# A two-layer hybrid attention step in fp32 on one Trainium2 core: RMS norms by half tiles, squared and summed beside the products before them

## The chip, the cores and the metric

The kernel runs on one core of a Trainium2 chip, as one launch. The metric is device time in microseconds (us); lower is better. Everything is fp32 apart from a few masks.

## The reference, cut to what matters

A trunk of two layers works on 512 prompt tokens and 8 sample tokens, 1024 channels each. The change concerns the RMS norm alone, which is applied five times: before the mixers and before the feed-forward part in both layers, and once at the end.

```python
def rmsnorm(x, g):
    xf = x.astype(jnp.float32)
    y = xf * lax.rsqrt(jnp.mean(xf * xf, axis=-1, keepdims=True) + RMS_EPS)
    return (y * g.astype(jnp.float32)).astype(x.dtype)
...
for i in range(DEPTH):
    h = rmsnorm(x, norm_mix_g[i])      # then all input projections read h
    x = x + merge_branches(...)        # ends in the product with w_out
    h = rmsnorm(x, norm_ffn_g[i])      # then gate and up read h
    x = x + swiglu(h, ...)             # ends in the product with w_down
y = rmsnorm(x, norm_final_g)
```

The loop is a summary; the rest of the layer (three attention branches over a paged past, gates, log-forget values) is as before in every respect.

## The kernel before, in words

**Layout.** The residual stream lies transposed in `xT`: 8 tiles of 128 channels by 520 tokens. A norm needs, for each token, the sum of squares over all 8 tiles and 128 partitions. The normalised stream goes to `hT`. [...]

**Order of work.** Five engines run hand-written programs that meet at semaphores. TensorE (PE), ScalarE (ACT) and VectorE (DVE) each run, per layer, norm 0, `project`, `compress`, `attend`, `merge`, norm 1, `ffn`. SyncE (SP) issues all loads in one fixed order: weights come in chunks of up to 2 MB through a ring of three slots, and a slot is loaded again once its last reader has signalled. GpSimd (POOL) scales probabilities, and forms sums and differences of weight blocks, in `merge`, `out`, `ffn` and `down`; these are two-input operations from SBUF.

**Products by seven.** The large products are done as a 2x2 block scheme with 7 products in place of 8 (helper `seven`, L1034; its `product` at L1042 is 4 matmuls of 260 columns). For the output projection and for gate and up it runs the groups f_1, f_11, d, f_u, f_22, f_21, f_12, each for q = 0 and 1. The d group multiplies a weight sum (POOL) with the difference of two quarters of the input, for `ffn` the tile BT[0], made by `first_sum` (L1936) on DVE; `later_sums` makes the other three (L1868 to L1870). The output projection runs `seven` twice (hf = 0, 1), and DVE adds each finished product to `xT` (L1922).

**Down projection** (`long`, L1163): four columns n = 0 to 3, each of seven products of 11 matmuls, p_1, p_2, d, p_6, p_3, p_7, p_4. DVE adds each to `xT` (L1991). The last one, p_4, completes tile 2n+1, half 0.

**The norm.** ACT squares whole tiles of 520 columns (L1234) into two buffers; PE multiplies each with a matrix of ones, two matmuls a tile (L603, L604), 16 in all, which adds over partitions and, in PSUM, over tiles; ACT takes two square roots (L1237); for each half DVE takes a reciprocal (L1594) and writes 8 tiles of `hT` (L1597, `scalar_tensor_tensor` with the gain). In the norm before `ffn` DVE makes `first_sum` after half of the second half's tiles. `project` computes its tile 0 first for token half 0 and then for half 1 (L653), waiting tile by tile of `hT`; its other tiles take both halves (L648, L649), and the first rotation is L626. At the very end PE transposes `hT` back (L582), which is then stored.

At the start SP loads constants and x, PE transposes x, DVE copies it to `xT` (L1585, L1586), and the first 2 MB of input weights follow (L464).

## Time and profile before

| | us |
|---|---|
| median of 3 runs | 2884.73 |
| lowest and highest | 2883.32, 2887.96 |
| the profiled execution, its own time | 2888.6 |
| its span, first to last instruction | 2886.8 |
| PE busy | 2584.5 (90%) |
| DVE, ACT, POOL busy | 897.1, 538.7, 638.0 |
| mean granted PE clock | 0.935 of full |

In the trace's views a line shows when a group of equal instructions started, how long it lasted, and in brackets how long its engine had been idle and who released it. A PE matmul record of 260 columns lasts 0.38 us, but the next starts 0.22 us after it.

### The profile page before, as it was taken

How to read it: one execution, taken by the hardware profiler on the slowest of the kernel's cores; microseconds unless marked ns; L12 is line 12 of the kernel's file. 1: busy time of each engine (PE TensorE's matmuls, PEld its weight loads, DVE VectorE, ACT ScalarE, POOL GpSimd, SP SyncE). 2: the span in 40 equal slices, each digit the busy share in tenths (PEclk: the TensorE clock that was granted, in tenths of full speed). 3: DMA queues.
4: the chain of work that ended last, by engine and by line, in shares of the span. 5: the costliest groups of instructions: out<-in, count | busy, mean ns of one | idle time of the engine just before them, and what ended most of it. 6: DMA issues, size and time to landing. Idle time of an engine off the chain costs nothing.

```text
span 2886.8 us, 43032 instructions
## 1 busy us (share of the span) xinstructions
PE 2584.5 (90%) x13546; PEld 1991.7 (69%) x13546; DVE 897.1 (31%) x1801; ACT 538.7 (19%) x1356; POOL 638.0 (22%) x564
## 2 busy tenths in 40 slices
PE   5997788877899999999999878888689999999997
PEld 4885544444588878888888664444357887888886
DVE  2203455421222432233131145552112334223412
ACT  1013222212222111110010232222141220111100
POOL 0000012111132424443300001121111242444431
PEclk8999789877999999999999998997789999999998
DMA  6242334245122212222514233341532222222120
GB/s 190 82 127 73 91 103 120 72 117 156 67 88 88 88 59 88 88 70 71 161 52 137 62 105 100 110 125 40 171 101 88 87 79 68 87 82 83 64 81 30
DMA packets 288295, 270.89 MB, mean 94 GB/s; under 512 B 50882, under 2 KB 249746, under 8 KB 287810
## 3 DMA queue, kind: packets, MB, share of 16 engines
q1 hardware_dynamic: 271266, 258.43, 29.2%
q10 hardware_dynamic: 16800, 9.61, 1.1%
q8 instruction: 119, 1.95, 0.3%
q14 instruction: 110, 0.90, 0.1%
HBM read 258.36 MB, written 17.97 MB: 96 GB/s over the span
## 4 chain that ended last, share of the span: by engine, by line
PE 77%; SPq 8%; issue 5%; DVE 5%; ACT 2%; POOL 1%; DMA 1%; ACTq 0%; DVEq 0%; POOLq 0%
PE ps L1042 32%; PE ps L1163 8%; PE ps L582 6%; PE ps L648 5%; PE ps L649 5%; SPq L557 3%; PE ps L938 3%; PE ps L863 2%; PE ps L802 2%; SPq L554 2%; POOL ring L1495 1%; PE ps L759 1%; PE ps L614 1%; PE ps L613 1%; PE ps L716 1%
## 5 line engine op out<-in xcount | busy, mean ns | idle before, releaser
L1495 POOL TENSOR_SCALAR ring<-ring,rr,gnat 128x31 f32<-128x31 f32 (+2 forms) x192 | 100.6, 534 | 1063.8 <-DVE rr L1713 1063.8
L1042 PE MATMUL ps<-hT,ring 128*128 128x260 f32 x1344 | 307.2, 386 | 8.2 <-DVE hT L1597 8.2
L1042 PEld LDWEIGHTS ps<-hT,ring 128*128 128x128 f32 x1344 | 258.2, 192 | 49.4 <-DVE hT L1597 9.0
L582 PE MATMUL ps<-cst,units 128*128 128x128 f32 x960 | 161.3, 302 | 61.2 <-ACT arena L1314 16.8
L1042 PE MATMUL ps<-hT,units 128*128 128x260 f32 x928 | 213.2, 382 | 0.0
L648 PE MATMUL ps<-hT,ring 128*128 128x260 f32 x672 | 202.4, 383 | 0.0
L649 PE MATMUL ps<-hT,ring 128*128 128x260 f32 x672 | 202.1, 382 | 0.0
L1042 PEld LDWEIGHTS ps<-hT,units 128*128 128x128 f32 x928 | 176.3, 190 | 27.1
L582 PEld LDWEIGHTS ps<-cst,units 128*128 128x128 f32 x960 | 114.6, 152 | 103.9 <-ACT arena L1314 38.0
L582 PE MATMUL ps<-cst,ring 128*128 128x128 f32 (+1 forms) x464 | 104.7, 314 | 75.9 <-POOL ring L1495 36.8
L1042 PE MATMUL ps<-arena,units 128*128 128x260 f32 x704 | 157.9, 382 | 0.0
L582 PEld LDWEIGHTS ps<-cst,ring 128*128 128x128 f32 (+1 forms) x464 | 54.9, 147 | 138.6 <-issue 72.5
L1042 PEld LDWEIGHTS ps<-arena,units 128*128 128x128 f32 x704 | 133.8, 190 | 20.5
L1788 DVE COPY arena<-ps 128x512 f32<-128x512 f32 x176 | 120.0, 687 | 88.4 <-PE ps L582 86.6
L649 PEld LDWEIGHTS ps<-hT,ring 128*128 128x128 f32 x672 | 127.7, 190 | 19.6
L648 PEld LDWEIGHTS ps<-hT,ring 128*128 128x128 f32 x672 | 126.3, 191 | 18.3
L1532 POOL TENSOR_TENSOR units<-ring 128x512 f32<-128x512 f32 x44 | 59.8, 1358 | 338.4 <-PE ps L1042 338.4
L1510 POOL TENSOR_TENSOR units<-ring 128x512 f32<-128x512 f32 x32 | 40.5, 1267 | 385.5 <-PE ps L1042 270.8
L1441 ACT ACTIVATE arena<-ps 128x260 f32<-128x260 f32 x132 | 51.1, 387 | 362.5 <-PE ps L1042 362.5
L1006 PE MATMUL ps<-units,arena 128*32 128x256 f32 x256 | 87.9, 506 | 33.2 <-DMA units<-in_cache_sb_kv 25.6
L1700 DVE TENSOR_REDUCE nm<-ps 128x2 f32<-128x256 f32 (+2 forms) x112 | 72.8, 650 | 140.4 <-PE ps L768 132.9
L1338 ACT ACTIVATE ring<-ps,nm 128x128 f32<-128x128 f32 (+2 forms) x224 | 100.3, 454 | 21.7 <-DVE nm L1700 21.2
(319 smaller groups left out, 4381.5 us busy)
## 6 DMA issues: line engine op xcount, KB each, us to landing
ring<-in_w_in SPq DMA_DIRECT2D x20, 2048.0 KB, 7.9
units<-in_cache_fox_kv SPq DMA_DIRECT2D x256, 128.0 KB, 2.2
units<-in_cache_sb_kv SPq DMA_DIRECT2D x256, 128.0 KB, 2.2
ring<-in_w_ffn_gate SPq DMA_DIRECT2D x22, 1024.0 KB, 5.4
ring<-in_w_ffn_up SPq DMA_DIRECT2D x22, 1024.0 KB, 8.0
ring<-in_w_ffn_down SPq DMA_DIRECT2D x16, 1408.0 KB, 6.2
units<-in_cache_nsa_cmp_kv SPq DMA_DIRECT2D x128, 128.0 KB, 2.6
units<-in_cache_nsa_sel_kv SPq DMA_DIRECT2D x256, 64.0 KB, 1.8
```

The costliest lines, as they stand in the source:

```text
L557: dma(slot[:, j * cols:(j + 1) * cols], rows(name)[l * NPOOL + pg][:, c0:c0 + cols]).then_inc(sem, 16)
L582: return nc.tensor.transpose(o, i, ident[0:n, 0:n])
L648: mm(ps[:, 2 * (i % 2), 0:H2], w[:, k, j * P:(j + 1) * P], hT[:, k, 0:H2], start=k == 0, stop=k == KD - 1)
L649: last = mm(ps[:, 2 * (i % 2) + 1, 0:H2], w[:, k, j * P:(j + 1) * P], hT[:, k, H2:T], start=k == 0, stop=k == KD - 1)
L938: mm(ps[lo, bank, :], qa, KT[0][:, i % 2, :], start=first, stop=True, skip_group_check=True).then_inc(sems["smm_a"], 1)
L1006: fox = mm(bank[64:96, 0:256], PTf[:, 4 * h + j, :], sf[:, j, :], start=h == 0 and j == 0, **sk)
L1042: last = mm(ps[:, bank, 0:H2], w[:, k, :], a[:, k, :], start=first and k == 0, stop=True, skip_group_check=True)
L1163: last = mm(ps[:, bank, 0:H2], w[:, k, :], x[k] if x is D2 else x[:, k, :], start=first and k == 0, stop=True, skip_group_check=True)
L1338: last = fn(Pb[:, n % 2, hh, 0:w], ps[:, hh, 0:w], ACT.Exp, bias=nm[:, n % 2, hh:hh + 1], accum_out=sm[:, n % 2, hh:hh + 1])
L1495: last = nc.gpsimd.tensor_scalar(p, p, one, gnat[:, i, c:c + 1], ALU.mult, ALU.mult)
L1700: v.tensor_reduce(nm[:, n % 2, :], ps[:, 0:2, 0:w], AX.X, ALU.max, negate=True).then_inc(sems["nm_ready"], 1)
L1788: v.tensor_copy(KT[s][:, i % 2, :], bank).then_inc(sems["kt_ev"], 1)
```

## The change

**Squares by half tiles.** ACT now squares 16 half tiles of 260 columns per norm, in the order in which the products before complete them (`HALVES`), each as soon as its last add has been made. DVE adds 12 of them into one running sum per token half (`accumulate`); the first square of a half is written straight into the sum, and the last is left to PE.

**PE's part** shrinks from 16 matmuls to 4: `total` multiplies the running sum and the last square of one half with ones. One half's `total` is put inside the product ahead of the norm (between the two f_12 products of the output projection; at k = 5 of the last p_4), the other behind the first product that follows (f_1 of `ffn`; the first 8 matmuls of `project`).

**The norm itself** begins with the half whose squares are complete; DVE makes the very last residual add after two tiles of that half (`early`). `project` computes tiles 0 and 1 for half 1 and then for half 0. The norm before a layer is now issued at the end of the layer before. At the start, x goes to another place, and `posT` is copied after the norm. The change's short description also names an overlap of the last two stick-breaking heads with the up projections; the kernel before has one in its plan (`in_order`), and no edit touches it.

```diff
+HALVES = ([(2 * n + c, h, name, k) for n in range(4)
+           for c, h, name, k in ((0, 0, "r_2", n + 1), (0, 1, "x_upd", 2 * n + 1), (1, 1, "r_d", n + 1), (1, 0, "x_upd", 2 * n + 2))],
+          [(4 * hf + 2 * q + c, h, name, k + q) for hf in range(2)
+           for c, h, name, k in ((0, 0, "x_11", 2 * hf + 1), (1, 1, "d_22", 2 * (NMG + hf) + 1), (1, 0, "x_upd", 4 * hf + 1), (0, 1, "x_upd", 4 * hf + 3))
+           for q in range(2)])
...
+class Squares:
...
+        self.half = [x[1] for x in HALVES[w]]
+        ends = [[e for e in range(16) if self.half[e] == h] for h in range(2)]
+        self.first, self.last = [x[0] for x in ends], [x[-1] for x in ends]
+        held = [e for e in range(16) if e not in self.first]
+        self.place = {e: i % 4 for i, e in enumerate(held)}
+        summed = [e for e in held if e not in self.last]
+        self.nth = {e: i + 1 for i, e in enumerate(summed)}
+        self.before = {e: held[i - 4] for i, e in enumerate(held) if i >= 4}
+        self.previous = {e: max([f for f in summed if f < e and self.half[f] == self.half[e]], default=None) for e in summed}
+        self.all_summed = [max(self.nth[e] for e in summed if self.half[e] == h) for h in range(2)]
...
+            def total(l, w, h):
+
+                sums, bank = SQUARES[w], 6 * w + h
+                pe.wait_ge(sems["sq_used"], at(pe, "sq_used", l, 12 * w + sums.all_summed[h]))
+                mm(ps[:, bank, 0:H2], C("ones")[:, 0:P], sqsum[:, h], start=True, stop=False)
+                pe.wait_ge(sems["sq_ready"], at(pe, "sq_ready", l, 16 * w + sums.last[h] + 1))
+                mm(ps[:, bank, 0:H2], C("ones")[:, 0:P], sq[:, sums.place[sums.last[h]]], start=False, stop=True).then_inc(sems["sum_ps"], 1)
...
+                    for k in range(KD if i >= 2 else 0):
...
-                        for k in range(KD):
-                            pe.wait_ge(sems["h_ready"], at(pe, "h_ready", l, t * KD + k + 1))
-                            last = mm(ps[:, t, 0:H2], w[:, k, 0:P], hT[:, k, t * H2:(t + 1) * H2], start=k == 0, stop=k == KD - 1)
-                    last.then_inc(sems["proj_ps"], 1)
+                    for t in (1, 0) if i == 0 else ():
+                        for m in range(2):
+                            for k in range(KD):
+                                if m == 0:
+                                    pe.wait_ge(sems["h_ready"], at(pe, "h_ready", l, (1 - t) * KD + k + 1))
+                                last = mm(ps[:, 2 * m + t, 0:H2], w[:, k, m * P:(m + 1) * P], hT[:, k, t * H2:(t + 1) * H2], start=k == 0, stop=k == KD - 1)
+                            if t == 0:
+                                last.then_inc(sems["proj_ps"], 1)
+                            elif m == 0:
+                                total(l, 0, 0)
+                    if i >= 2:
+                        last.then_inc(sems["proj_ps"], 1)
...
                     product(3 * q, w1[q][:, :, lo], x(0), True).then_inc(sems["f_1"], 1)
+                    if q == 0:
+                        between("first")
...
                     product(3 * q + 2, ws[q][3], x(3)).then_inc(sems["f_12"], 1)
+                    if q == 0:
+                        between("last")
...
-                    seven(l, 2 * (NMG + hf), w1, w2, [[MS[q][0], MS[q][1], w1[q][:, :, P:2 * P], MS[q][2]] for q in range(2)], 4, merged, OT_, free)
+                    seven(l, 2 * (NMG + hf), w1, w2, [[MS[q][0], MS[q][1], w1[q][:, :, P:2 * P], MS[q][2]] for q in range(2)], 4, merged, OT_, free,
+                          lambda part: total(l, 1, 0) if hf and part == "last" else None)
...
-                            if bank == "b":
-                                pe.wait_ge(sems["rs_ready"], at(pe, "rs_ready", l, 4))
...
-                    seven(l, 2 * (NMG + NOUT + j), w1, w2, ws, 8, quarter, BT, free)
+                    seven(l, 2 * (NMG + NOUT + j), w1, w2, ws, 8, quarter, BT, free,
+                          lambda part: total(l, 1, 1) if j == 0 and part == "first" else None)
...
+                    long(f, w2[:, :, hi], D4, True, lambda k: total(l.next, 0, 1) if n == 3 and k == 5 else None).then_inc(sems["p_4"], 1)
+
+            total(0, 0, 1)
...
-            norm(DEPTH, 0)
+            total(DEPTH, 0, 0)
...
-                    fn(sq[:, k % 2, :], xT[:, tile, :], ACT.Square).then_inc(sems["sq_ready"], 1)
...
-                for t in range(2):
-                    fn(rs[:, t * H2:(t + 1) * H2], ps[:, t, 0:H2], ACT.Sqrt, bias=epsb[:, 0:1], scale=1.0 / D).then_inc(sems["rs_ready"], 1)
...
+                def square(e):
+                    t, h, name, n = HALVES[w][e]
+                    act.wait_ge(sems[name], at(act, name, l, n) if w else count(act, l, PER[name], n))
+                    if e in sums.before:
+                        act.wait_ge(sems["sq_used"], at(act, "sq_used", l, 12 * w + sums.nth[sums.before[e]]))
+                    fn(sq[:, sums.place[e]] if e in sums.place else sqsum[:, h], xT[:, t, h * H2:(h + 1) * H2], ACT.Square).then_inc(sems["sq_ready"], 1)
+
+                def take_root(n, h):
+                    act.wait_ge(sems["sum_ps"], at(act, "sum_ps", l, 2 * w + n))
+                    fn(rs[:, h], ps[:, 6 * w + h, 0:H2], ACT.Sqrt, bias=epsb[:, 0:1], scale=1.0 / D).then_inc(sems["rs_ready"], 1)
+
+                for e in range(15):
+                    square(e)
+                take_root(1, 0 if w else 1)
+                square(15)
+                take_root(2, 1 if w else 0)
...
+            norm(0, 0)
...
+                norm(l.next, 0)
...
+                    dve.wait_ge(sems["sq_used"], at(dve, "sq_used", l, 12 * w + sums.nth[sums.previous[e]]))
+                to = sqsum[:, sums.half[e]]
+                v.tensor_tensor(to, to, sq[:, sums.place[e]], ALU.add).then_inc(sems["sq_used"], 1)
...
+                v.tensor_copy(xT[:, k, 0:SEQ], ps[:, 2 * (k % 2), :]).then_inc(sems["x_upd" if k % 2 else "r_2"], 1)
+                v.tensor_copy(xT[:, k, SEQ:T], ps[:, 2 * (k % 2) + 1, 0:NS]).then_inc(sems["r_d" if k % 2 else "x_upd"], 1)
+                if k:
+                    accumulate(0, 0, 2 * k - 2)
+                    accumulate(0, 0, 2 * k - 1)
+
+            def norm(l, w, g, early=lambda: None, amid=lambda: None):
+                for n, t in enumerate((0, 1) if w else (1, 0)):
+                    dve.wait_ge(sems["rs_ready"], at(dve, "rs_ready", l, 2 * w + n + 1))
+                    own(v.reciprocal(ps[:, 6 + t, 0:H2], rs[:, t]), "rinv_ok", l, 2 * w + n + 1)
                     for k in range(KD):
                         to = slice(t * H2, (t + 1) * H2)
                         v.scalar_tensor_tensor(hT[:, k, to], xT[:, k, to], g(k), ps[:, 6 + t, 0:H2], ALU.mult, ALU.mult).then_inc(sems["h_ready"], 1)
...
+                        if n == 0 and k == 1:
+                            early()
+                        if n and k == KD // 2 - 1:
                             amid()
...
                     add("f_1", 0, 0, a, "c_1")
-                    add("f_11", 0, 0, b, None, "c_1")
+                    add("f_11", 0, 0, b, "x_11", "c_1")
+                    if hf:
+                        squares(-2, 0)
                     add("f_u", 0, 1, a, "c_u")
+                    squares(0, 2)
                     add("f_22", 1, 1, a, "c_3")
                     add(None, 1, 1, d, "d_22", "c_3")
-                    add("f_21", 1, 0, a, "x_upd")
-                    add("f_12", 0, 1, d, "x_upd", "c_u")
+                    add("f_21", 1, 0, a, "x_upd", None, (0,))
+                    squares(2, 4)
+                    add("f_21", 1, 0, a, "x_upd", None, (1,))
+                    squares(4, 5)
+                    add("f_12", 0, 1, d, "x_upd", "c_u", (0,))
+                    squares(5, 7 if hf else 6)
+                    if hf:
+                        norm(l, 1, lambda k: gl[:, 0, k:k + 1], lambda: add("f_12", 0, 1, d, "x_upd", "c_u", (1,)), lambda: first_sum(l))
+                    else:
+                        add("f_12", 0, 1, d, "x_upd", "c_u", (1,))
...
                     add(x12, d).then_inc(sems["x_upd"], 1)
+                    accumulate(l.next, 0, 4 * n)
+                    accumulate(l.next, 0, 4 * n + 1)
...
                     add(x22, d).then_inc(sems["r_d"], 1)
-                    dve.wait_ge(sems["p_4"], at(dve, "p_4", l, n + 1))
-                    add(x21, f).then_inc(sems["x_upd"], 1)
...
+                    def finish():
+                        dve.wait_ge(sems["p_4"], at(dve, "p_4", l, n + 1))
+                        add(x21, f).then_inc(sems["x_upd"], 1)
+
+                    if n < 3:
+                        accumulate(l.next, 0, 4 * n + 2)
+                        finish()
+                        accumulate(l.next, 0, 4 * n + 3)
+                    else:
+                        norm(l.next, 0, lambda k: gl[:, 1, k:k + 1], finish)
+
+            norm(0, 0, lambda k: gam[:, 0, k:k + 1])
...
+                dve.wait_ge(sems["h_ready"], at(dve, "h_ready", l, 2 * KD))
+                v.tensor_copy(gl[:, :, :], gam[:, bass.ds(2 * i + 1, 2), :])
```

## Rows read from the trace of the kernel before

**Rows 1.** The page: busy time by engine, and the chain that ended last by engine

```profile
PE 2584.5 (90%) x13546; PEld 1991.7 (69%) x13546; DVE 897.1 (31%) x1801; ACT 538.7 (19%) x1356; POOL 638.0 (22%) x564
...
PE 77%; SPq 8%; issue 5%; DVE 5%; ACT 2%; POOL 1%; DMA 1%; ACTq 0%; DVEq 0%; POOLq 0%
```

**Rows 2.** Timeline, layer 0's second norm: start, length, engine, line, op, count, [idle before]

```profile
1024.65 1.92 PE L1042 MATMUL ps<-PT,vnat 128*128 128x260 f32 x8
1024.94 0.42 DVE L1922 TENSOR_TENSOR xT<-xT,ps 128x260 f32<-128x260 f32 x1 [1.43 <-PE ps L1042]
...
1026.87 1.27 POOL L1532 TENSOR_TENSOR units<-ring 128x512 f32<-128x512 f32 x1 [19.73 <-PE ps L1042]
...
1027.48 0.64 ACT L1234 ACTIVATE arena<-xT 128x520 f32<-128x520 f32 x1 [27.83 <-PE ps L604]
...
1033.34 0.60 PE L604 MATMUL ps<-arena,cst 128*128 128x260 f32 x2
1033.98 0.85 ACT L1237 ACTIVATE arena<-ps,epsb 128x260 f32<-128x260 f32 x2 [1.24 <-PE ps L604]
...
1034.49 1.79 DVE L1594 RECIPROCAL ps<-arena 128x260 f32<-128x260 f32 x1 [7.36 <-ACT arena L1237]
1035.85 1.26 POOL L1539 TENSOR_TENSOR units<-ring,units 128x512 f32<-128x512 f32 x1 [0.16 <-POOL units L1536]
1036.31 3.26 DVE L1597 SCALAR_TENSOR_TENSOR hT<-xT,gl,ps 128x260 f32<-128x260 f32 x8
...
1038.04 8.69 PE L1042 MATMUL ps<-hT,ring 128*128 128x260 f32 x32 [4.10 <-DVE hT L1597]
...
1041.50 0.39 ACT L1441 ACTIVATE arena<-ps 128x260 f32<-128x260 f32 x1 [6.68 <-PE ps L1042]
1043.00 1.24 DVE L1936 TENSOR_TENSOR arena<-hT 128x1040 f32<-128x1040 f32 x1
...
1046.56 7.18 PE L1042 MATMUL ps<-arena,units 128*128 128x260 f32 x32
```

**Rows 3.** Timeline, the same stretch of layer 1

```profile
2427.98 1.92 PE L1042 MATMUL ps<-PT,vnat 128*128 128x260 f32 x8
...
2451.36 7.18 PE L1042 MATMUL ps<-arena,units 128*128 128x260 f32 x32
```

**Rows 4.** Timeline, end of layer 0 and first projections of layer 1

```profile
1444.28 4.79 PEld L1163 LDWEIGHTS ps<-arena,ring 128*128 128x128 f32 x22
...
1444.70 1.22 DVE L1991 TENSOR_TENSOR xT<-xT,ps 128x260 f32<-128x260 f32 x3 [3.94 <-PE ps L1163]
...
1460.07 8.97 PE L653 MATMUL ps<-hT,ring 128*128 128x260 f32 x32 [2.91 <-DVE hT L1597]
...
1475.66 0.41 PEld L626 LDWEIGHTS ps<-PT,cst 128*128 128x128 f32 x2
```

**Rows 5.** Timeline, the final norm

```profile
2847.39 4.79 PEld L1163 LDWEIGHTS ps<-arena,ring 128*128 128x128 f32 x22
...
2868.04 2.39 PE L582 MATMUL ps<-cst,hT 128*128 128x128 f32 x10 [7.90 <-DVE hT L1597]
```

**Rows 6.** Timeline, the first projection of layer 0

```profile
49.58 9.68 PE L653 MATMUL ps<-hT,ring 128*128 128x260 f32 x32 [7.73 <-DMA ring<-in_w_in]
...
65.89 0.19 PEld L626 LDWEIGHTS ps<-PT,cst 128*128 128x128 f32 x1
```

**Rows 7.** A stretch: busy time by engine, then granted clock as a share of full

```profile
1038.00:1040.00 2.00, 1.96 (x5) 1.58 (x6) 2.00 (x5) 0.00 (x0) 0.00 (x0) 0.50 0.00 0
```

**Rows 8.** Duration in ns, min/median/max, of one DVE line

```profile
L1951 DVE TENSOR_TENSOR PT<-arena x66: 421/423/3120, 1058.0 to 2715.0; 128x260 f32<-128x260 f32 x66
```

**Rows 9.** Timeline, POOL beside that line's longest one

```profile
1309.89 3.17 POOL L1548 TENSOR_TENSOR units<-ring 128x1408 f32<-128x1408 f32 x1 [15.15 <-PE ps L1042]
1310.22 3.12 DVE L1951 TENSOR_TENSOR PT<-arena 128x260 f32<-128x260 f32 x1
```

**Rows 10.** Waits: engine, line, who released it, us in total, times, longest

```profile
DVE xT L1991 <- PE ps L1163: 214.5, 44, 9.2
```

More of the change, by code:

```diff
@@ L165, in __init__ @@
         self.more = more
+        self.next = Layer(more + 1) if more == 0 else None
 def w_dmas(ch):
@@ L344, in build @@
         VALUE_SEM = {"selv": "v_sel", "winv": "v_sel", "fxv": "v_fox", "sbv": "v_sb"}
-        CREDIT = {name: PER[name] for name in ("p_6", "p_4", "v_sel", "v_fox", "v_sb")}
+        CREDIT = {name: PER[name] for name in ("p_6", "p_4", "v_sel", "v_fox", "v_sb", "r_2", "r_d")}
         BASE = {"x_upd": KD}
@@ L1035, in so, with seven @@
                 last.then_inc(sems["so_ps"], 1)
-            def seven(l, g, w1, w2, ws, base, x, t, free):
+            def seven(l, g, w1, w2, ws, base, x, t, free, between=lambda part: None):
                 def product(bank, w, a, first=False):
@@ L1460, in _ @@
                 l = layer[0] = in_layers(act, i)
-                norm(l, 0)
                 project(l)
@@ L1913, in merge, with add @@
                     g = 2 * (NMG + hf)
-                    def add(name, t, h, bank, to, n=None):
-                        for q in range(2):
+                    def add(name, t, h, bank, to, n=None, only=(0, 1)):
+                        for q in only:
                             x = xT[:, 4 * hf + 2 * q + t, h * H2:(h + 1) * H2]
@@ L2018, in _ @@
                 merge(l)
-                norm(l, 1, lambda k: gl[:, 1, k:k + 1], lambda: first_sum(l))
                 ffn(l)
             assert chain[0] == DVE_CHAIN, chain
-            layer[0] = DEPTH
-            chain[0] = 0
-            norm(DEPTH, 0, lambda k: gam[:, 2 * DEPTH, k:k + 1])
             yp = PT[:, 0:8, :].rearrange("p a b -> p (a b)")[:, 0:4096].rearrange("p (t d) -> p t d", t=TT)
```

68 lines of the change are left out of this document (28 added, 40 removed).

## The prediction

> **What bounds the kernel now.** I read the page first [rows 1]: PE is busy 90% of the span and holds 77% of the chain that ended last. So time is won where PE stands still or does work that can go. The five norms are such places, and I read the timeline around each.
>
> The norm before `ffn` shows the pattern [rows 2]. PE begins the last product of the output projection (f_12, q = 1) at 1024.65. 1.75 us later, at 1026.40, it turns to ones-matmuls, and the last pair of these starts at 1033.34. ACT's root starts at 1033.98, DVE's reciprocal at 1034.49, the first tile of `hT` at 1036.31, and PE resumes at 1038.04. It then does four products, f_1 and f_11, and begins d at 1046.56. From 1024.65 to 1046.56 are 21.91 us. A product is 8 records, and one comes every 0.22 us (22 weight loads in 4.79 us, [rows 4]): 4 matmuls of 0.44, or 1.75 us. So five useful ones are 8.8 us and the norm costs PE 13.1 us. Layer 1 takes 23.38 us for the same stretch [rows 3].
>
> At the layer boundary [rows 4] the last p_4 begins at 1444.28, and project's tiles 0 and 1 are done at 1475.66: 31.38 us, of which 4.83 + 14.04 (11 and 32 matmuls) are useful. The final norm [rows 5] puts 20.65 us between the start of p_4 and the first transpose back. The first norm differs: there PE waits until 49.58 for the first weights, a DMA in the trace, after 7.73 us of idle [rows 6].
>
> **The change, part by part.** My links, all from rows 2, are these. From the start of a `total`'s weight load to the root is 1.30 us: 0.22, one matmul of 0.44, and the 0.64 from 1033.34 to 1033.98. From root to reciprocal is 0.51, from reciprocal to first `hT` tile 1.82. A further tile costs 0.41, its result is there 0.48 after its start, and an add to `xT` takes the same pipeline slot of 0.41. A `total` costs PE two matmuls, 0.88 us. The square of a half tile is not in the trace; it lies between ACT's copy of the same shape, 0.39 at 1041.50 [rows 2], and the 0.64 of a whole tile, at 1027.48. I take 0.39, the same engine and width.
>
> *Norm before `ffn`, layer 0.* The first `total` is put at 1024.43 (loads run 0.22 ahead of matmuls) and f_12 q = 1 moves to 1025.3. ACT must square the tile added at 1024.94 to 1025.36 before it takes the root, which therefore starts at 1025.8. Reciprocal at 1026.3, first tile at 1028.15; four tiles and the one late add in their midst are done at 1028.15 + 4 x 0.41 + 0.48 = 1030.3. PE resumes there instead of at 1038.04, 7.7 us earlier, after 2.8 us of standing still. Then f_1 (1.75), the second `total` from 1032.05, and f_1, f_11, f_11: PE is free at 1038.2. The second half's chain gives root 1033.35, reciprocal 1033.85, first tile 1035.7, four tiles 1037.4, and then `first_sum` of 1.24, as at 1043.00 in rows 2. POOL is late next: its weight sums for `ffn` start when f_12 ends and last 10.24 us (1026.87 to 1037.11). They move with f_12 by 0.88, to end at 1038.0. A DVE instruction with two SBUF operands waited for POOL's [rows 8, 9]: 3.12 us in place of 0.42. So I let `first_sum` wait till 1038.0 and end at 1039.3, d begins at about 1039.5, and 7.0 us are saved; in layer 1, whose old stretch is 1.47 longer, 8.5. The clock takes some back. PE had stood still for 4.10 us at 1038.04, and the granted clock of the next 2 us was 0.50, the 1.2 GHz level [rows 7]; the four products took 8.3 us (1038.04 to 1046.34, the load of d) instead of 7.0. After the 2.91 us ahead of 1460.07 [rows 4], 32 records took 8.97 us where 7.18 is usual, as at 1046.56 [rows 2]. At half rate, f_1 needs up to 3.5 us and the second `total` up to 1.76, which lies on the chain: up to 2.6 us each. I take 0.9 each. Sum for both: 15.5 - 1.8 = 13.7 us.
>
> The Trainium skill, "TensorE: Matmul & The Clock Gate", section "Why this matters for your kernels", says to leave no idle gap of some length between matmul bursts, or the clock goes to its lower level. Rows 7 agree that it fell after the old gap. By that rule alone the shorter gap would cost nothing and the sum would be 1.8 us larger.
>
> *Boundary.* The `total` inside p_4 loads at 1444.28 + 5 x 0.44 = 1446.47; the square it needs follows the adds at 1444.70 to 1445.92 and is done at 1446.35, so nothing waits. Root 1447.8, reciprocal 1448.3, first tile 1450.1. PE ends p_4 at 1450.0 (0.88 later than before) and starts project at 1450.6; it stops again before its third matmul, as the late add lies between tiles 2 and 3 (0.3), and ends the first 8 matmuls at 1454.5. The second `total` follows; its chain of 1.30 + 0.51 + 1.82 + 0.48 = 4.1 us is covered by that `total` and 8 matmuls, 4.4. Without this cover 0.3 us at most would come back. It and three more times 8 matmuls make: 1454.5 + 0.88 + 24 x 0.44 = 1465.9, against 1475.66. Saved: 9.8 us.
>
> *Final norm.* The same chain from 2847.39: first tiles 2853.2, late add done 2854.5, its square 2854.9, `total`, root 2856.2, but DVE writes the first half until 2857.0; reciprocal to 2858.8, tile at 2859.3, and PE transposes from there instead of 2868.04. Saved: 8.7 us. The transposes after it stay at low clock; were they not, up to 1.5 us more.
>
> *First norm.* PE starts at 49.58 in any case. It had no norm left after that; now one `total` of 0.88 stands between its products. Loss: 0.9 us. DVE's 12 adds ahead, 12 x 0.42 = 5 us, slow PE's transposes of x and are hidden by the 7.73 us of waiting; were that cover gone, they would cost their 5.
>
> *The 60 new adds on DVE* (12 per norm) and ACT's 80 half squares in place of 40 whole ones (80 x 0.39 = 31 us against 40 x 0.64 = 26, on an engine that waits for these adds) I cost at nothing. An add takes 0.42 free of POOL [rows 8]. In the down projection DVE idles 214.5 / 44 = 4.9 us before each add that waits [rows 10]. Behind a waiting add stand DVE's residual adds, and PE's bank releases behind these. The Trainium skill, "SBUF — State Buffer", calls the port pair that DVE and GpSimd share an exclusive lock, held for the full instruction; rows 8 and 9 agree, and it speaks against this change. Two adds per column fall into POOL's 3.17 us sums. Each can wait that long, and 4.9 us of idle hold it. If the cover is gone, a column's two cost up to 2 x 2.7 = 5.4 us.
>
> *Moved copies* (`posT`, `gl`, `posL`, `bfl`) of 0.2 each wait behind 16 tiles; PE needs none. No DMA is added; the weights of tile 0 at the boundary are issued by 1436.1 before and after, and the next chunk's issue moves with p_4 by 0.88. SP's later loads are keyed to PE's progress, so they shift along.
>
> **Sum.** 13.7 + 9.8 + 8.7 - 0.9 = 31.3 us. The profiled execution took 2888.6 (span 2886.8 and 1.8 around it); it would take 2857.3. It stands 3.9 above the median of the runs, 2884.73, from which I get 2853.4.
>
> **Rivals.** (a) *The lock decides.* If, in the three columns followed by POOL's work, both layers, 5.4 us per column reach PE, 32.4 us come back: no gain, 2885.8. For it: rows 9. Against: 4.9 us of idle before each add. It is this rival by the skill's rule above. Chance 0.03. (b) *Slower.* Each of the 60 sums costs DVE its 0.42 and a wait for a square of up to 0.64, in line with a residual add that PE waits for: 60 x 1.06 = 63.6, less 31.3, or 32 us slower, 2917. It decides where these waits outgrow the idle before a residual add. Chance 0.03. (c) *Cache loads hide the boundary gain.* If layer 1's page loads (SP's queue is 8% of the chain, rows 1) do not come earlier, 9.8 us are lost: 2863. Against: their issue follows PE's signals. Chance 0.07. (d) *The clock* falls for longer after the shorter gaps: 3.4 us more at both norms before `ffn` and at the boundary 1.8, what rows 4 lost there (8.97 less 7.18): 2858.6. Chance 0.12. (e) The description also names stick-breaking heads; no edit touches them, so that part does nothing, and the forecast counts nothing for it.
>
> **How the numbers follow.** Forecast 0.75, rivals as above. Bounds on the forecast: no clock loss and quicker transposes, 34.6 us saved, 2850.1; full clock loss (3.4 more) and 0.64 for a square (some 2 in all), 25.9 saved, 2858.8. The runs spread by 1.4 below and 3.2 above their median, and (c) lies at 2863. Range 2846 to 2865. What a measurement can tell from no change is about 0.2%, 5.8 us. Faster by more: 0.75 + 0.12 + 0.07 = 0.94; within: 0.03; slower: 0.03.
>
> **What would show it.** Right: PE's record of ones-matmuls shrinks from 16 to 4 per norm; about 15 us instead of 21.9 and 23.4 from f_12's `total` to d; about 21.6 instead of 31.4 at the boundary; 12 instead of 20.65 at the end; in the down projection, adds of up to 3 us beside POOL but no PE wait behind them. Wrong: a PE wait on DVE in the down or output projection, granted clock of 0.50 at the boundary, or an attention stage that grows by what the norms gave.

## The result, and where the time went

| | before | after |
|---|---|---|
| median of the timed runs, us | 2885.31 (4 runs) | 2856.78 (4 runs) |
| lowest and highest | 2883.32, 2887.96 | 2851.67, 2859.41 |
| the profiled execution; its span | 2888.6; 2886.8 | 2859.41; 2857.6 |
| mean granted PE clock of that execution | 0.935 | 0.931 |

The ratio of the medians is 0.9903, 95% interval 0.989 to 0.9915: 28.5 us faster, where 31.3 were forecast. The before column has one timed run more than the three that the forecast started from. The page, busy time by engine and the chain by engine:

```profile
PE 2562.0 (90%) x13426; PEld 1973.9 (69%) x13426; DVE 932.8 (33%) x1861; ACT 545.2 (19%) x1396; POOL 641.4 (22%) x564
...
PE 76%; SPq 8%; DVE 6%; issue 5%; ACT 2%; POOL 2%; DMA 1%; ACTq 0%; DVEq 0%; POOLq 0%
```

PE has 120 records less than in [rows 1]: five norms, each with 24 fewer (16 ones-matmuls became 4, and every matmul of 260 columns leaves two records). It is busy for 22.5 us less. DVE has 60 instructions more, the new sums.

**The norm before `ffn`, layer 0** (timeline; start, length, engine, line, op, count, idle time before). It answers to [rows 2]:

```profile
1023.54 1.92 PE L1080 MATMUL ps<-PT,units 128*128 128x260 f32 x8
...
1025.29 0.60 PE L635 MATMUL ps<-arena,cst 128*128 128x260 f32 x2
...
1026.46 0.46 ACT L1281 ACTIVATE arena<-ps,epsb 128x260 f32<-128x260 f32 x1
...
1027.03 1.78 DVE L1657 RECIPROCAL ps<-arena 128x260 f32<-128x260 f32 x1
...
1029.64 0.42 DVE L1987 TENSOR_TENSOR xT<-xT,ps 128x260 f32<-128x260 f32 x1
...
1030.90 3.71 PE L1080 MATMUL ps<-hT,ring 128*128 128x260 f32 x8 [2.81 <-DVE hT L1660]
...
1034.44 0.60 PE L635 MATMUL ps<-arena,cst 128*128 128x260 f32 x2
...
1036.03 1.78 DVE L1657 RECIPROCAL ps<-arena 128x260 f32<-128x260 f32 x1 [3.60 <-ACT arena L1281]
...
1039.56 1.24 DVE L2016 TENSOR_TENSOR arena<-hT 128x1040 f32<-128x1040 f32 x1
...
1040.93 0.92 PE L1080 MATMUL ps<-arena,units 128*128 128x260 f32 x3 [0.19 <-DVE arena L2016]
```

The reader sees two short pairs of ones-matmuls where 16 stood, one ahead of f_12's second product and one behind f_1's first; the late add to `xT` in the midst of the tiles (1029.64); PE's stand (idle time) of 2.81 us; and f_1 behind it, whose 8 records take 3.54 us up to the next `total` instead of 1.75.

**The layer boundary**, against [rows 4]:

```profile
1438.76 2.35 PE L1206 MATMUL ps<-arena,ring 128*128 128x260 f32 x10
...
1440.96 0.60 PE L635 MATMUL ps<-arena,cst 128*128 128x260 f32 x2
...
1442.03 0.48 ACT L1281 ACTIVATE arena<-ps,epsb 128x260 f32<-128x260 f32 x1 [1.32 <-PE ps L637]
...
1445.11 3.81 PE L686 MATMUL ps<-hT,ring 128*128 128x260 f32 x16 [0.49 <-DVE hT L1660]
...
1449.64 10.68 PE L686 MATMUL ps<-hT,ring 128*128 128x260 f32 x48
...
1460.16 0.60 PE L657 MATMUL ps<-PT,cst 128*128 128x260 f32 x2
```

PE works nearly without a break: its stand shrank from 2.91 to 0.49 us, and 21.40 us lie between the start of p_4 and the first rotation.

**The final norm**, against [rows 5], where 20.65 us lay between p_4's first load and the transposes:

```profile
2827.81 2.36 PE L1206 MATMUL ps<-arena,ring 128*128 128x260 f32 x10
...
2836.92 1.78 DVE L1657 RECIPROCAL ps<-arena 128x260 f32<-128x260 f32 x1
...
2839.27 1.11 PE L611 MATMUL ps<-cst,hT 128*128 128x128 f32 x4 [3.35 <-DVE hT L1660]
```

It is 11.46 from p_4's first matmul to the first transpose, against 20.43 before by the same two marks.

**A ledger.** I cut every trace of this study at the same PE instructions. At the boundary and at the end the parts of one kernel repeat to 0.3 us, mostly to 0.05. The stretch from f_1 to d in the kernel before takes one of two values, 8.52 or 9.98, and not by layer: layer 1 has the longer one in the first trace and the shorter one in e5. The first projection scatters by 1 us. The whole repeats worst, since timed runs of one kernel differ by 5 to 17 us. So the account below goes by parts. Before: four traces (the first one, e5, e9, e10), after: three (after, e1, e11); means in us.

| stretch | before | after | change | forecast |
|---|---|---|---|---|
| first projection to first rotation | 16.00 | 16.96 | +0.96 | +0.9 |
| f_12 (q = 0) to d, layers 0 and 1 | 2 x 24.4 | 2 x 17.39 | -14.0 | -13.7 |
| boundary, p_4 to the first rotation | 31.17 | 21.40 | -9.8 | -9.8 |
| final norm, p_4 to the transposes | 20.43 | 11.46 | -9.0 | -8.7 |
| **the five norms** | | | **-31.8** | **-31.3** |
| p_6 in the down projection, both layers | 2 x 4.02 | 2 x 4.75 | +1.5 | 0 |
| attention and output projection, layer 0 | 953.9 | 955.7 | +1.8 | 0 |
| the same, layer 1 | 951.1 | 953.6 | +2.5 | 0 |
| up to the first projection; from the last transposes on | 49.31; 18.80 | 50.10; 18.34 | +0.3 | 0 |
| up to p_6, both layers | 2 x 280.4 | 2 x 280.5 | +0.2 | 0 |
| **span** | 2883.7 | 2858.2 | **-25.5** | -31.3 |

The norms gave what was forecast. The stretch from p_6's end to the last p_4 is left out of the table; it is 112.65 us in every trace. Some 6 us were lost again in parts that no edit touches, and the experiments ask where.

### The profile page after: what moved, and what is told of

Same layout as the page of the kernel before. It is cut to its first block, busy times and chain, and to the rows that moved or that the text cites. A ratio compares the mean times of both kernels' runs of the same rounds, so it can differ in the third digit from the quotient of the medians.

```text
span 2857.6 us, 43023 instructions
## 1 busy us (share of the span) xinstructions
PE 2562.0 (90%) x13426; PEld 1973.9 (69%) x13426; DVE 932.8 (33%) x1861; ACT 545.2 (19%) x1396; POOL 641.4 (22%) x564
## 4 chain that ended last, share of the span: by engine, by line
PE 76%; SPq 8%; DVE 6%; issue 5%; ACT 2%; POOL 2%; DMA 1%; ACTq 0%; DVEq 0%; POOLq 0%
PE ps L1080 32%; PE ps L1206 8%; PE ps L611 6%; PE ps L679 5%; PE ps L680 5%; SPq L586 3%; PE ps L976 2%; PE ps L901 2%; PE ps L840 2%; POOL ring L1546 2%; SPq L583 2%; PE ps L797 1%; PE ps L645 1%; PE ps L644 1%; PE ps L686 1%
## 5 line engine op out<-in xcount | busy, mean ns | idle before, releaser
L1080 PE MATMUL ps<-hT,ring 128*128 128x260 f32 x1344 | 306.4, 385 | 5.6 <-DVE hT L1660 5.6
L1080 PEld LDWEIGHTS ps<-hT,ring 128*128 128x128 f32 x1344 | 257.0, 191 | 46.3 <-DVE hT L1660 6.4
L679 PE MATMUL ps<-hT,ring 128*128 128x260 f32 x640 | 193.6, 384 | 0.0
L680 PE MATMUL ps<-hT,ring 128*128 128x260 f32 x640 | 193.3, 384 | 0.0
L611 PEld LDWEIGHTS ps<-cst,units 128*128 128x128 f32 x960 | 113.5, 151 | 95.7 <-DVE arena L1853 31.8
L611 PE MATMUL ps<-cst,ring 128*128 128x128 f32 (+1 forms) x464 | 104.9, 315 | 78.4 <-POOL ring L1546 39.4
L1080 PEld LDWEIGHTS ps<-arena,units 128*128 128x128 f32 x704 | 133.6, 190 | 21.6 <-issue 1.2
L680 PEld LDWEIGHTS ps<-hT,ring 128*128 128x128 f32 x640 | 122.2, 191 | 18.9
L679 PEld LDWEIGHTS ps<-hT,ring 128*128 128x128 f32 x640 | 120.7, 192 | 17.6
L1949 DVE TENSOR_TENSOR vnat<-vnat,ps 128x260 f32<-128x260 f32 x72 | 30.5, 425 | 226.4 <-ACT vnat L1470 119.9
```

What stands on the lines that cost most here:

```text
L611: return nc.tensor.transpose(o, i, ident[0:n, 0:n])
L679: mm(ps[:, 2 * (i % 2), 0:H2], w[:, k, j * P:(j + 1) * P], hT[:, k, 0:H2], start=k == 0, stop=k == KD - 1)
L680: last = mm(ps[:, 2 * (i % 2) + 1, 0:H2], w[:, k, j * P:(j + 1) * P], hT[:, k, H2:T], start=k == 0, stop=k == KD - 1)
L1080: last = mm(ps[:, bank, 0:H2], w[:, k, :], a[:, k, :], start=first and k == 0, stop=True, skip_group_check=True)
```

## The experiments

For each kernel the median is given, the ratio to the kernel before and its 95% interval. The kernel before, run beside them, had medians of 2887.73 (11 runs, beside e1 to e4), 2884.2 (15, e5 to e8), 2888.54 (1, e9 to e11) and 2886.67 (7, e12). The intervals of e1, e2, e3, e4, e6 and e7 overlap each other and the changed kernel's, so the timed runs do not tell the changed kernel and the variants e2, e3, e4, e6 and e7 apart. What is said of these rests on the parts of their traces, one trace of two layers each. e8 lies clear of e1, and e12 of every kernel but e8.

**e1, e5, e9, e10, e11: both kernels again**, with no edit, to learn how far a part moves by itself.

> The changed kernel once more, on the chip and in the hours of the three runs beside it: the level that they are read against. Theory: the norms give 32 us and about 3 us of that goes to two stretches that differ from run to run, the granted clock after PE's 2.8 us stand in the down projection and DMA waits in the attention stage. Then this run is again 27 to 31 us under the kernel before, its five norm stretches repeat within 0.2 us apart from those at half clock, and the attention stretch of layer 1 (first rotation to first sum before the feed-forward norm, 952.1 before and 954.0 after) comes out elsewhere between 950 and 956. Rival: the change itself slows the attention stage by 1.9 us; then it is 954 again, within 0.3.

> The kernel before, traced once more. Theory: the 1.9 us that layer 1's attention stretch seemed to cost (952.2 against 950.3 us from the first rotation to the last product ahead of the norm) and the 1.7 us of the down projection (p_6 at half clock in layer 0, not in layer 1) are chance of one execution. The four traces of the changed kernel's family so far gave 950.9 to 953.6 for the same stretch. So this trace should lie anywhere in 950 to 954 there, and p_6 of either layer may come out at 3.2 or at 4.6 to 4.9 us. The five norm stretches repeat within 0.1 us, up to 1.5 us of low clock. Rival: the change slows the attention; then it is 950.3 again, within 0.3.

> A third trace of the kernel before, for the attention stretch of layer 1 alone. It was 950.34 and 949.92 us before, and 950.7 to 953.6 (mean 952.3) in eight traces of kernels with the change. Theory: chance of the execution, as in layer 0, where the same stretch is 952 to 959 in all of them; this trace and the next then fall between 950 and 954, at least one of them above 951.5. Rival: the change costs layer 1's attention 2 us; both come out under 950.6.

> A fourth trace of the kernel before, with the same expectation as the third: between 950 and 954 for the attention stretch of layer 1 by theory, under 950.6 by the rival.

> A third trace of the changed kernel as it is. Its five norm stretches repeat within 0.1 us (17.39 from the first f_12 product to d, 21.40 at the boundary, 11.46 at the end), p_6 is at 3.2 or at 4.6 to 4.9, and the attention stretch of layer 1 lies between 950 and 954; by the rival it is above 951.9 again.

Measured: e1 2861.69, 0.9914 [0.9899, 0.9928]; e5 2883.82, 0.9999 [0.9989, 1.0008]; e9, e10 and e11, one run each, 2886.26, 2884.11 and 2861.51. Layer 1's stretch of attention and output projection was 950.34, 949.92, 953.65 and 950.42 in the kernel before, and 952.23, 952.70 and 955.80 in the changed one. So it moves by 4 us with no edit at all, which is more than the difference that was to be explained. The means still differ by 2.5. One part of it does not scatter within these two kernels: from the first rotation to the first load of `w_up_nsa` layer 1 took 135.6 us in all four traces of before and 137.3 in all three of after. It is not bound to the change either: e2, e6 and e7, which keep most of it, took 135.6 or 135.7 there, and 950.7 to 951.7 for the whole stretch. e12 takes that up.

**e2: the new sums twice.** Each of the 60 sums is followed by a second DVE instruction of the same shape, which waits for the first and leaves the values as they are.

```diff
-                v.tensor_tensor(to, to, sq[:, sums.place[e]], ALU.add).then_inc(sems["sq_used"], 1)
+                own(v.tensor_tensor(to, to, sq[:, sums.place[e]], ALU.add), "twice", l, 12 * w + sums.nth[e])
+                v.tensor_tensor(to, to, sq[:, sums.place[e]], ALU.max).then_inc(sems["sq_used"], 1)
```

> Each of DVE's 60 sums of squares is followed by a second pass over the same operands (a maximum, which leaves the value as it is), so DVE's new work and its claims on the port shared with POOL are doubled. Theory (the adds are covered by DVE's idle time): only the sum just ahead of the reciprocal in the norm before ffn lies on the path, so +0.5 us at each of the two, +1 us in all, under 2 us. Rival a (the port lock decides): two more adds per column wait up to 2.7 us each beside POOL, and with the first two they outgrow 4.9 us of idle: up to 5.4 us for each of six columns, +15 to +32 us. Rival b (every sum is on the path): 60 times 0.45, +27 us.

Measured: 2858.62, 0.9905 [0.9884, 0.9926]. The group of the sums in the changed kernel (busy, mean ns, idle before), and POOL beside one of the longest second sums in e2:

```profile
L1644 DVE TENSOR_TENSOR arena<-arena 128x260 f32<-128x260 f32 x60 | 39.4, 664 | 10.6 <-ACT arena L1277 10.4
```

```profile
1408.52 3.36 POOL L1600 TENSOR_TENSOR units<-ring 128x1408 f32<-128x1408 f32 x1
1408.88 3.27 DVE L1645 TENSOR_TENSOR arena<-arena 128x260 f32<-128x260 f32 x1
```

A sum takes 0.42 us alone and 0.66 on average in the changed kernel, where the longest took 1.88; a second sum of e2 took up to 3.3 where POOL adds weights. DVE worked 72 us more than in the changed kernel (63.8 + 47.9 less 39.4), and the down stretches from p_6's end to p_4 stayed at 112.65 us to the hundredth. What it cost on PE's waits lies at the norms before `ffn`: 7.83 for 7.36 up to f_1, where one sum stands in line ahead of the reciprocal, of which 0.2 is left at d. The boundary and the final norm took the same 21.40 and 11.46. One stretch grew all the same, by 1.4 us in each layer: p_6, behind a stand as long as before.

```profile
1319.95 6.38 PE L1206 MATMUL ps<-units,hT 128*128 128x260 f32 x14 [2.78 <-DVE xT L2072]
```

The granted clock was 0.50 for nearly all of these 6.2 us, in the changed kernel for the first 3 or so of its 4.7. Why it stayed down longer in e2 was not followed up; e8 shows what p_6's stand has to do with it.

The Trainium skill, "SBUF — State Buffer", section "SBUF: two separate sides", has the port pair of DVE and GpSimd held by one of them for a whole instruction. The rows of 1408 agree; the rule decides nothing here, as the idle time ahead of the residual adds, 178.4 us in 42 waits in the changed kernel, holds it:

```profile
DVE xT L2071 <- PE ps L1206: 178.4, 42, 9.2
```

**e3: PE kept at work in the stand** of the norm before `ffn`. Six matmuls of the constant ones into a bank not in use, behind the output projection; their result is never read.

```diff
                 merge(l)
+                fill(1, 6)
                 ffn(l)
...
+            def fill(bank, n):
+                for i in range(n):
+                    mm(ps[:, bank, 0:H2], C("ones")[:, 0:P], C("ones")[:, 0:H2], start=True, stop=True)
```

> In both norms before ffn PE fills its 2.8 us stand with 6 matmuls of ones (2.6 us, into a bank that is not read), so that the clock has no reason to fall. Theory: the fall costs 1.8 us of f_1 and the second total at 1.2 GHz, and the chain behind them: granted clock 1.00 from f_1 on, f_1 x8 in 1.9 us instead of 3.7 and 3.4, and first_sum earlier by 0.9 us (it then runs into POOL's last weight sum, which ends at 1038.7) to 1.7. So -1.8 to -3.4 us in all, of 2857. Rival: the clock was granted down for another reason, or falls all the same; then f_1 keeps its length and nothing changes, within 1 us.

Measured: 2859.98, 0.9906 [0.9892, 0.9921]; by the ledger d starts 1.05 us earlier in both layers. First the changed kernel in the 2 us behind its stand, then e3 (per stretch: PE, PEld, DVE, ACT, POOL, granted clock, DMA), and e3's timeline:

```profile
1030.90:1032.90 2.00, 2.00 (x5) 1.61 (x6) 1.53 (x4) 0.00 (x0) 1.83 (x2) 0.52 1.09 375
```

```profile
1030.00:1032.00 2.00, 2.00 (x9) 1.77 (x10) 1.52 (x4) 0.00 (x0) 1.83 (x2) 1.00 1.09 379
```

```profile
1029.99 2.02 PE L1085 MATMUL ps<-hT,ring 128*128 128x260 f32 x8 [0.19 <-DVE hT L1666]
...
1036.47 1.27 POOL L1596 TENSOR_TENSOR units<-ring,units 128x512 f32<-128x512 f32 x1 [0.16 <-POOL units L1593]
1036.96 1.88 DVE L2022 TENSOR_TENSOR arena<-hT 128x1040 f32<-128x1040 f32 x1
...
1038.97 3.33 PE L1085 MATMUL ps<-arena,units 128*128 128x260 f32 x14 [0.82 <-DVE arena L2022]
```

The clock was 1.00, the 2.4 GHz level, instead of 0.52, and f_1 began at full rate. The clock's price is shown, and the next limit with it: now `first_sum` reaches its turn while POOL's last sum runs, takes 1.88 us instead of 1.24, and PE waits 0.82 us on it. That is why 1.05 came back of the 1.8 that f_1 had lost: `first_sum`'s longer time is 0.64 of the rest. The Trainium skill's rule on idle gaps, in "TensorE: Matmul & The Clock Gate", section "Why this matters for your kernels", would have had the shorter stand cost nothing; row 1030.90 says otherwise.

**e4: the second `total` ahead of f_1.**

```diff
                     if q == 0:
                         between("first")
                     free("a", q)
                     product(3 * q, w1[q][:, :, lo], x(0), True).then_inc(sems["f_1"], 1)
-                    if q == 0:
-                        between("first")
```

> The second total of the norm before ffn is issued ahead of f_1 instead of behind it. Its square is done at 1030.6 and f_1 begins at 1030.9, so the total fills the stand's last 0.3 us and puts f_1 off by 0.6. Theory: what sets the begin of d (1040.93) is the chain second total, root, reciprocal, four tiles, first_sum, which now starts 3.5 us earlier but must wait for DVE's first eight tiles (1032.4) and for POOL; d then begins when PE is through f_1 and f_11, at 1030.65 + 0.88 + 7.0 + 1.5 for the low clock = 1040.1: -0.8 us per norm, -1.7 us in all. Rival: PE's own work sets it, so that a total moved within it changes nothing, 0 within 0.5 us; or the low clock doubles the total too, +0.5 us.

Measured: 2856.29, 0.9891 [0.9874, 0.9908]. The stretch takes 16.35 us for 17.39. PE reaches f_1 0.5 us later (7.89 for 7.36; 7.97 in layer 1), since the pair waits for its square, but the second chain no longer stands behind a slow f_1. Here the port went to DVE, and POOL waited:

```profile
1035.54 1.24 DVE L2016 TENSOR_TENSOR arena<-hT 128x1040 f32<-128x1040 f32 x1
1035.63 2.29 POOL L1587 TENSOR_TENSOR units<-units,ring 128x512 f32<-128x512 f32 x1
```

**e6: the norm's start undone at the boundary and at the end**: `total` behind p_4, and the last residual add ahead of the norm. The sums by halves stay.

```diff
-                    long(f, w2[:, :, hi], D4, True, lambda k: total(l.next, 0, 1) if n == 3 and k == 5 else None).then_inc(sems["p_4"], 1)
+                    long(f, w2[:, :, hi], D4).then_inc(sems["p_4"], 1)
+                    if n == 3:
+                        total(l.next, 0, 1)
...
-                        norm(l.next, 0, lambda k: gl[:, 1, k:k + 1], finish)
+                        finish()
+                        norm(l.next, 0, lambda k: gl[:, 1, k:k + 1])
```

> At the end of both layers the first total is issued behind p_4 instead of at its sixth matmul, and the last residual add comes ahead of the norm instead of within it; half tiles and sums on DVE stay. Theory (the place of the total is what starts root and reciprocal early): first tile 2.6 us later, less the 0.4 of the add, so the boundary (21.40 from p_4 to the first rotation) grows by 2.3, and by up to 1.8 more if the clock falls in PE's stand of 3.2 us; the final norm (11.46) grows by 2.2. Together +4.5 to +6.3 us. Rival: DVE's 8 tiles per half set the length anyway, so that the place of the total gives at most 1 us.

Measured: 2859.7, 0.9913 [0.9898, 0.9927]; by the ledger +3.95 at the boundary and +2.30 at the end.

```profile
1433.15 4.99 PE L1206 MATMUL ps<-arena,ring 128*128 128x260 f32 x22
...
1441.92 5.34 PE L686 MATMUL ps<-hT,ring 128*128 128x260 f32 x16 [2.91 <-DVE hT L1662]
```

So 2.4 us of stand and 1.5 of clock (5.34 for 3.81) come back at the boundary. Of the 9.8 us there, the placement is worth 3.95; of the other 5.8, the 12 ones-matmuls that are gone make 5.3 (at 0.44); the last 0.5 was not followed up.

**e7: the interleaving undone in the norm before `ffn`**: all of the output projection, the late add, both `total`s, then the tiles.

```diff
-lambda part: total(l, 1, 0) if hf and part == "last" else None
+lambda part: None
...
-lambda part: total(l, 1, 1) if j == 0 and part == "first" else None
+lambda part: None
...
                 merge(l)
+                total(l, 1, 0)
+                total(l, 1, 1)
                 ffn(l)
...
-                        norm(l, 1, lambda k: gl[:, 0, k:k + 1], lambda: add("f_12", 0, 1, d, "x_upd", "c_u", (1,)), lambda: first_sum(l))
+                        add("f_12", 0, 1, d, "x_upd", "c_u", (1,))
+                        norm(l, 1, lambda k: gl[:, 0, k:k + 1], lambda: None, lambda: first_sum(l))
```

> In the norm before ffn both totals are issued behind the output projection and ahead of f_1, and the last residual add ahead of the norm. Theory: f_1 begins 1.5 us later (8.9 after the first f_12 product instead of 7.36), but no total is left between f_1 and d and the second chain starts earlier, so d comes at 17.4, where it is now (17.39), if f_1 runs at the low clock, and at 15.9 if the two shorter stands leave the clock up: 0 to -1.5 us per norm. Rival (interleaving is what gave the gain here as well): d comes later by the 1.5 of f_1 and by the totals' 0.9, +2.4 us per norm.

Measured: 2855.86, 0.9901 [0.9887, 0.9914]. By the ledger the stretch takes 15.76 us for 17.39, in both layers: **by these two traces this part of the change is a loss of 1.6 us each** (the timed runs, 0.9901 against 0.9903, cannot show 3 us), and the gain at the norm before `ffn` comes from the rest, the halves and the sums on DVE that take the place of 12 ones-matmuls.

```profile
1024.17 0.71 PE L637 MATMUL ps<-arena,cst 128*128 128x260 f32 x2 [0.44 <-ACT arena L1279]
...
1027.40 7.28 PE L1080 MATMUL ps<-hT,ring 128*128 128x260 f32 x32 [2.52 <-DVE hT L1662]
```

PE stands 0.44 and 2.52 us, reaches f_1 1.3 us later, and then does 32 records in 7.28 us at full rate with nothing in between; in the changed kernel the stand of 2.81 brought the clock down.

**e8: e3 and e4 together, and PE kept at work in one more stand**, in the down projection ahead of p_6.

```diff
                     long(d, DS[0], D1)
+                    if n == 0:
+                        fill(5, 6)
```

> All that the traces of the runs before point to: 6 matmuls of ones in PE's stand in both norms before ffn, the second total ahead of f_1, and 6 more matmuls of ones in the 2.8 us stand ahead of p_6 in the first column of the down projection. Theory (the clock follows PE's stands; with it up and the total ahead, PE's own work sets d): d at 14.9 after the first f_12 product instead of 17.39, so -2.5 per norm; p_6 x14 in 3.2 us instead of 4.6 to 4.9, -1.6 per layer. Together -8.2 us against the changed kernel. Rival: the waits on DVE, first_sum against POOL's weight sums above all, set d at 16.3 as in the two runs that did one of these alone, so -2.1 at the norms and -5.3 in all.

Measured: 2851.36, 0.9875 [0.9859, 0.989]. By the ledger 14.91 us for 17.39 in both layers, and 3.17 for p_6 in both. The stand ahead of p_6 is in both kernels and differs by 0.02 us. In the kernel before, layer 0 (14 records of p_6 up to 1331.85), and in the changed one:

```profile
1326.99 5.02 PE L1163 MATMUL ps<-units,hT 128*128 128x260 f32 x14 [2.80 <-DVE xT L1991]
...
1331.85 1.92 PE L1163 MATMUL ps<-arena,hT 128*128 128x260 f32 x8
```

```profile
1321.44 4.84 PE L1206 MATMUL ps<-units,hT 128*128 128x260 f32 x14 [2.78 <-DVE xT L2071]
```

Before, p_6 took 4.86 us in four of eight layers traced and 3.18 in the other four, behind the same stand. This is e5's layer 0:

```profile
1323.39 3.33 PE L1163 MATMUL ps<-units,hT 128*128 128x260 f32 x14 [2.78 <-DVE xT L1991]
```

Wherever it took 3.18, the stretch from f_1 to d in the same layer had taken 9.98, and where 4.86, 8.52. In the changed kernel and its variants without this fill it took 4.6 to 4.9 in 14 layers and 6.2 in e2's two: the lower clock followed in 16 of 16. So 0.7 us a layer went there on average, for a stand that the change did not touch.

**e12: e8, and the gate row broken up.** The gates are 40 matmuls of 28 columns, one row behind a projection tile. Here five of them follow each of that tile's eight pairs.

```diff
+                    gates = []
+                    if i == WINV:
+                        pe.wait_ge(sems["rope_done"], at(pe, "rope_done", l, ROPE.index(WINK)))
+                        gates = [(t, k) for t in range(TT + 1) for k in range(KD)]
                     for k in range(KD if i >= 2 else 0):
                         mm(...)
                         last = mm(...)
+                        for t, g in gates[5 * k:5 * k + 5]:
+                            gate = mm(...)
...
                     if i == WINV:
-                        pe.wait_ge(sems["rope_done"], at(pe, "rope_done", l, ROPE.index(WINK)))
-                        for t in range(TT):
-                            for k in range(KD):
-                                mm(...)
-                        for k in range(KD):
-                            last = mm(...)
-                        last.then_inc(sems["gate_ps"], 1)
+                        gate.then_inc(sems["gate_ps"], 1)
```

> Same kernel as e8 (ones-matmuls in both stands, total ahead), and in both layers the gates' 40 matmuls of 28 columns (80 records) no longer stand in one row behind the product of tile WINV but five behind each of its eight pairs. In all traces so far the row lasts 10.8 to 11.7 us, the granted clock is 1.00 for its first 4 us and 0.50 from there to some 5 us behind it, although PE is busy all along; this is where the layer 1 project stage differs between the kernels (135.62 us against 137.28 from the first rotation to the first load of w_up). Theory A (the row of short matmuls itself lets the clock fall): with long matmuls between, the clock stays at 1.00; the 80 records take 0.09 us each, 7.1 in place of 11.7 in e8, and the rotation and products behind them 2.2 in place of 4.5: 135.62 or 137.3 becomes about 130.5 in each layer, and the span is 11 to 13 us below e8's 2853.4, near 2841. Theory B (the fall has another cause, such as the stand of 0.72 on DVE behind the row, or the place in the program): the clock falls as before, the stage stays at 135.6 to 137.3 or grows by up to 3 us, since the product of 7.0 us now lies in the slow stretch too.

Measured: 2841.21, 0.9846 [0.9824, 0.9869], the best of this study: 45 us below the kernel before, 15.6 below the changed one. The timed runs put it 10 us below e8, with intervals that touch; the row's own time below is the firmer number. Layer 1 in the kernel before, then in the changed kernel, then in e12:

```profile
1538.57 9.94 PE L660 MATMUL ps<-ring,hT 128*128 128x28 f32 x64
1548.43 0.92 PE L662 MATMUL ps<-ring,hT 128*8 128x28 f32 x16
1550.07 1.24 PE L626 MATMUL ps<-PT,cst 128*128 128x260 f32 x2 [0.72 <-DVE lfs L1624]
```

```profile
1522.85 10.91 PE L698 MATMUL ps<-ring,hT 128*128 128x28 f32 x64
...
1538.07 1.08 PE L679 MATMUL ps<-hT,ring 128*128 128x260 f32 x2
1538.93 0.91 PE L680 MATMUL ps<-hT,ring 128*128 128x260 f32 x2
```

```profile
1516.15 1.20 PE L692 MATMUL ps<-ring,hT 128*128 128x28 f32 x10
...
1521.07 0.71 PE L662 MATMUL ps<-PT,cst 128*128 128x260 f32 x2 [0.72 <-DVE lfs L1699]
```

And the stretches, before and e12:

```profile
1543.88:1544.88 1.00, 1.00 (x6) 1.00 (x7) 0.00 (x0) 0.00 (x0) 0.00 (x0) 0.50 0.00 0
```

```profile
1515.64:1517.64 2.00, 2.00 (x16) 1.89 (x15) 0.00 (x0) 0.00 (x0) 0.00 (x0) 1.00 0.00 0
```

In the row PE counts as busy all of the time (matmul ends are modelled in the trace) and still falls to 0.50, the 1.2 GHz level. All 26 rows traced ahead of e12, in 13 traces, do so, 2.8 to 6 us after the row's begin, and they last 9.1 to 12.0 us; the expectation had 10.8 to 11.7 and 4 us for all. With long matmuls between, the clock stays at 1.00 through the row and the same wait of 0.72 behind it, in both layers, so the wait is not its cause. From the first rotation to the load of `w_up_nsa` it is 131.5 us in both layers, against 137.3 in e8: 5.8 each. In the other traces this stretch took 134.0 (twice), 135.6 or 137.3, so against the kernel before's layer 1 the gain is 4.1. I had expected 130.5; ten short records take 1.03 us, not 0.9. The other 5 us of the 16.6 between the two spans lie elsewhere in the attention stretch, within its scatter.

This row also holds layer 1's 1.65 us: in after it lasts 0.97 longer (10.91 for 9.94), and the first pair of products behind it, 1.08 and 0.91 until the clock is up, takes 0.7 more than before. Layer 0 shows either value in both kernels, and e2, e6 and e7 show the shorter one in layer 1. Where in the row the clock falls and rises differs by kernel and layer; why the row is the longer one in all three traces of after was not settled.

## Why the prediction was right, and where its steps were off

**The sum.** 31.3 us were forecast for the norms and 31.8 measured by the traces, so the mechanism held, and the sizes too, apart from two at the norm before `ffn` that made up for each other. The time, forecast 2853.4, came out at 2856.8, in the range; the 6 us that the ledger lost outside the norms were in no term of the forecast, and the range covered them without having priced them.

**The norm before `ffn`.** Root, reciprocal and first tile followed as worked out: PE resumed 5.82 us after the `total`'s load (forecast 1030.3 - 1024.43 = 5.87), after the 2.8 us of standing that had been forecast. Two steps of the sum failed, and it was luck that they nearly cancelled. "I let `first_sum` wait till 1038.0": it did not wait for POOL, whose sums ended at 1038.7, since it came only at 1039.56. And "I take 0.9 each" for the clock was too little: f_1 took 3.54 us for 1.75, the second `total` came late by as much, and with it the second chain. The forecast had d held up by the lock (DVE waiting for POOL's port) and got the clock instead; d came 15.85 us after the `total`'s load, forecast 15.1 and 0.9 for the clock. e3 shows both: without the clock's fall 1.05 come back, and then the lock binds. The 1.5 us more that the forecast saved in layer 1 were no trait of that layer: in the traces of before either layer has the longer stretch, and the ledger's means share it out. What the forecast did not ask is whether the interleaving is worth its place at all. e7's traces say that it costs 1.6 us a layer here.

**Boundary and end.** Counted, as in the forecast, from p_4's first weight load (0.22 us ahead of its first matmul), the root was forecast at 3.5 and came at 3.48, the first product at 6.3 and 6.56, the first rotation's load at 21.6 and 21.39. At the end 11.9 were forecast for the transposes, 11.68 measured.

**The first norm** lost 0.96 us (forecast 0.9; single traces of one kernel scatter by 1 us here), and the adds ahead of it stayed behind the weights' DMA:

```profile
49.91 6.15 PE L686 MATMUL ps<-hT,ring 128*128 128x260 f32 x16 [16.77 <-DMA ring<-in_w_in]
```

**The new adds** were priced at nothing. e2 confirms it for PE's waits, for all but the one in each chain: doubled, they put f_1 off by 0.5 us and d by 0.2 at each norm before `ffn`. The 1.4 us a layer that e2 lost at p_6 are clock, and open.

**The rivals.** (a) and (b) fall with e2. (c) falls: layer 1's attention lost 2.5 us in the means, not 9.8. (d), the clock, was half right: 0.9 us more than the sum had at each norm before `ffn`, but nothing at the boundary, where no stand was left. What no part of the forecast had was the clock in places that the change does not touch: 1.5 us at p_6 and 1.65 in layer 1's gate row. The last 2.7 us or so of attention are no more than its scatter, and stay open. (e) stands: no stick-breaking head was touched, and nothing in the ledger asks for one.

## What to carry to other kernels

Price a norm between two products by what it takes from TensorE and by the stand it leaves, and follow each stand with the granted clock of the work behind it; a few matmuls with no reader in a stand of 2.8 us gave back 1.05 us (e3) and 1.6 (e8's p_6). Try interleaving against the plain order with the same sums: where it splits one stand into a stand and a slow product on the second chain, it loses. Look for the lower clock also where the engine is busy: a row of short matmuls spread among long ones was worth 4.1 to 5.8 us a layer, where the placement at the boundary was worth 3.95.

## What the hardware showed that was not expected

- A stand of 2.8 us ahead of p_6 was followed by the lower clock in 4 of 8 layers of the kernel before and in 16 of 16 of the changed kernel and its variants. In e2's two the stand was as long and the low clock lasted for nearly all of p_6's 6.2 us, instead of 3 us or so. A stand of 2.52, after one of 0.44, was not followed by it (e7).
- PE fell to 0.50 while the trace counts it busy without a gap, in a row of 80 records of 28 columns, in all 26 rows traced; the same 80 with long matmuls between ran at 1.00 (e12).
- Where DVE and POOL both read two operands in SBUF, either can be the one that waits: DVE 1.88 us for 1.24 beside POOL (e3), POOL 2.29 for 1.27 beside DVE (e4).
